# Low parts of streamed weight chunks: accumulating load onto the negated high part, in place of a subtraction

## The reference

```python
x = layer_norm(ALPHA * x + 0.5 * swiglu(x, ffn1_w_up, ffn1_w_down), ln1_g, ln1_b)
h, new_buf, S_new = mixer(x, ...)     # x @ w_in -> gates, short convolution, 4 retention heads,
                                      # y_conv = z @ w_conv_br, y_ret = o @ w_ret_br, m @ w_out
x = layer_norm(ALPHA * x + h, ln2_g, ln2_b)
x = layer_norm(ALPHA * x + 0.5 * swiglu(x, ffn2_w_up, ffn2_w_down), ln3_g, ln3_b)
```

## Time and profile before

| | us |
|---|---|
| median of 3 runs | 1780.68 (1778.77 to 1781.95) |
| span of the profiled execution | 1778.3 |
| stage: opening and first down product | 0 to 44.5 |
| rest of FFN 1 and its layer norm | 44.5 to 445 |
| quads of the input projection | 445 to 842 |
| last gates and convolution branch (chunks 32 to 42) | 842 to 932 |
| four heads (9 chunks each) | 932 to 1310 |
| output product, layer norm, first units of FFN 2 | 1310 to 1390 |
| rest of FFN 2, last layer norm | 1390 to 1778 |

### The profile page before, as it was taken

How to read it: one execution, slowest core, us unless ns; L and a number is a source line. 1 busy time by engine, 2 the same in 40 slices (tenths; PEclk the granted TensorE clock), 3 DMA queues, 4 the chain that set the end, 5 groups by cost and what they waited for, 6 DMA issues and landing times.

```text
span 1778.3 us, 26857 instructions
## 1 busy us (share of the span) xinstructions
PE 1766.5 (99%) x10776; PEld 1653.0 (93%) x10776; DVE 1286.1 (72%) x1708; ACT 653.3 (37%) x1120; POOL 551.6 (31%) x355
## 2 busy tenths in 40 slices
PE   9999999999999999999999999999999999999998
PEld 9989999898999999999998989898989989899997
DVE  7958485678788787777266777767867968485676
ACT  5425233243545454444105050514224325242343
POOL 3424242242232222221242323332343324233331
PEclk9999999999999999999999999999999999999999
DMA  7442423334443333433674858676963442324223
GB/s 275 136 137 72 143 78 130 126 94 178 148 148 127 115 128 99 139 98 95 243 247 159 313 198 296 214 265 222 351 264 118 129 154 86 131 79 135 90 89 107
DMA packets 87259, 282.61 MB, mean 159 GB/s; under 512 B 8672, under 2 KB 9056, under 8 KB 86880
## 3 DMA queue, kind: packets, MB, share of 16 engines
q1 hardware_dynamic: 48096, 172.77, 29.4%
q10 hardware_dynamic: 24784, 56.21, 8.7%
q0 software_dynamic: 14256, 51.91, 8.6%
HBM read 239.63 MB, written 42.28 MB: 159 GB/s over the span
## 4 chain that ended last, share of the span: by engine, by line
PE 94%; DVE 3%; DMA 1%; ACT 1%; issue 1%; DVEq 0%; ACTq 0%
PE ps L872 93%; PE ps L1348 1%; DMA out_ret_sample<-state 1%; DMA state<-in_state_ret 0%; DVE xl L1961 0%; DVE z L2277 0%; DMA opening<-in_opening 0%; DVE z L2380 0%; PE ps L1257 0%; DVE wql L1961 0%; ACT xh L1510 0%; ACT t L1900 0%; DVE t L2010 0%; DVE y L2415 0%; DVE tl L1961 0%
## 5 line engine op out<-in xcount | busy, mean ns | idle before, releaser
L872 PE MATMUL ps<-th,wql 128*128 128x320 f32 x1136 | 351.0, 309 | 0.0
L872 PE MATMUL ps<-th,wqh 128*128 128x320 f32 x1136 | 350.7, 309 | 0.0
L872 PE MATMUL ps<-tl,wqh 128*128 128x320 f32 x1136 | 350.0, 308 | 0.0
L773 POOL TENSOR_TENSOR wl<-raw,wh 128x1024 fp32r<-128x1024 f32 x100 | 262.8, 2628 | 133.9 <-DMA wh<-in_weights 81.8
L1510 ACT ACTIVATE pu<-ps 128x320 f32<-128x320 f32 x213 | 93.2, 438 | 515.8 <-PE ps L872 515.8
L1961 DVE TENSOR_TENSOR wql<-qraw,wqh 128x512 fp32r<-128x512 f32 x213 | 260.0, 1221 | 17.2 <-ACT wqh L1510 17.0
L872 PE MATMUL ps<-xh,wql 128*128 128x320 f32 x852 | 262.7, 308 | 0.2 <-DVE wql L1961 0.2
L872 PE MATMUL ps<-xl,wqh 128*128 128x320 f32 x852 | 262.7, 308 | 0.0
L872 PE MATMUL ps<-xh,wqh 128*128 128x320 f32 x852 | 262.6, 308 | 0.0
L786 POOL TENSOR_TENSOR quad_s<-qraw 128x512 f32<-128x512 f32 x71 | 96.7, 1362 | 478.8 <-DVE wql L1961 412.9
L1961 DVE TENSOR_TENSOR wql<-quad_s,wqh 128x512 fp32r<-128x512 f32 (+1 forms) x213 | 197.5, 927 | 44.2 <-ACT wqh L1510 43.4
(11 more groups left out here) (246 smaller groups left out, 3446.2 us busy)
## 6 DMA issues: line engine op xcount, KB each, us to landing
qraw<-in_quads SPq DMA_DIRECT2D x142, 512.0 KB, 3.6
raw<-in_weights SPq DMA_DIRECT2D x100, 512.0 KB, 3.9
wh<-in_weights POOLq DMA_DIRECT2D x92, 512.0 KB, 5.3
state<-in_state_ret ACTq DMA_DIRECT2D x32, 512.0 KB, 7.5
out_ret_sample<-state ACTq DMA_DIRECT2D x32, 512.0 KB, 6.4
state<-in_state_ret SPq DMA_DIRECT2D x16, 512.0 KB, 5.7
qk_scratch<-ctp SPq DMA_DIRECT2D x8, 640.0 KB, 5.6
swish_scratch<-ctp SPq DMA_DIRECT2D x6, 640.0 KB, 2.9
```

The costliest lines, as they stand in the source:

```text
L773: pool.tensor_tensor(w_lo(r), w_raw(r), w_hi(r).bitcast(f32), ALU.subtract).then_inc(chunk_split, 1)
L872: ins = nc.tensor.matmul(out, lhs, rhs, start=start, stop=stop, skip_group_check=adds)
```

## The change

For the 97 chunks that are not made by ScalarE, the plain load by SyncE is gone. GpSimd instead writes minus the high part into the low tile (a multiplication by -1), waits for that instruction's own semaphore, and issues a second load of the chunk with `accum_op=ALU.add` into the same tile: `-wh + w`. TensorE waits for the landing of that load (`low_loaded`, one semaphore per slot). `max_dma_last_dim=4 * D` lets one descriptor carry a row of 4 KB. SyncE no longer waits for the fourth chunk's plain load ahead of `z_scratch`, and ScalarE waits for the landing of chunk 25's low part ahead of the load of the norm's gains.

```diff
 def loads_of_slot(c):
-    return sum(SLOTS[e] == SLOTS[c] for e in range(FIRST_HI, c + 1))
+    return sum(SLOTS[e] == SLOTS[c] and e in BY_ACT for e in range(FIRST_HI, c + 1))
...
                 for _ in range(n):
                     c = ck.at
                     r = slot_of(c)
-                    slot_free(sync, c)
-                    sync.dma_start(w_raw(r), a["weights"][c]).then_inc(raw_loaded[r], 16)
+                    if c in BY_ACT:
+                        slot_free(sync, c)
+                        sync.dma_start(w_raw(r), a["weights"][c]).then_inc(raw_loaded[r], 16)
                     ck.add()
...
                 fourth = SECOND + FIRST_UNITS - 1
-                sync.wait_ge(raw_loaded[slot_of(fourth)], 16 * loads_of_slot(fourth))
...
                 c = ck.at
                 high(c + 1)
                 r = slot_of(c)
-                pool.wait_ge(raw_loaded[r], 16 * loads_of_slot(c))
                 if c in BY_ACT:
+                    pool.wait_ge(raw_loaded[r], 16 * loads_of_slot(c))
                     pool.wait_ge(hi_made, BY_ACT.index(c) + 1)
+                    pool.tensor_tensor(w_lo(r), w_raw(r), w_hi(r).bitcast(f32), ALU.subtract).then_inc(chunk_split, 1)
                 else:
                     pool.wait_ge(hi_loaded[r], 16 * high_loads_of_slot(c))
-                pool.tensor_tensor(w_lo(r), w_raw(r), w_hi(r).bitcast(f32), ALU.subtract).then_inc(chunk_split, 1)
+                    pool.tensor_scalar(w_lo(r), w_hi(r).bitcast(f32), -1.0, None, ALU.mult).then_inc(high_negated, 1)
+                    nk.add()
+                    pool.wait_ge(high_negated, nk())
+                    pool.dma_start(w_lo(r), a["weights"][c], accum_op=ALU.add,
+                                   max_dma_last_dim=4 * D).then_inc(low_loaded[r], 16)
                 ck.add()
...
             def chunk():
-                s = slot_of(ck.at)
+                c, s = ck.at, slot_of(ck.at)
                 ck.add()
-                if ck() > FIRST_HI:
-                    pe.wait_ge(chunk_split, ck(-FIRST_HI))
+                if c in BY_ACT:
+                    pe.wait_ge(chunk_split, BY_ACT.index(c) + 1)
+                elif c >= FIRST_HI:
+                    pe.wait_ge(low_loaded[s], 16 * high_loads_of_slot(c))
                 return s
...
-            act.wait_ge(chunk_split, FFN_CHUNKS - FIRST_HI)
+            act.wait_ge(low_loaded[slot_of(SECOND - 1)], 16 * high_loads_of_slot(SECOND - 1))
```

More of the change, by code:

```diff
@@ L485, in build_layer @@
         hi_loaded = [sem(f"hi_loaded{i}") for i in range(NSPL + 2)]
-        chunk_split = sem("chunk_split")
+        chunk_split, high_negated = sem("chunk_split"), sem("high_negated")
+        low_loaded = [sem(f"low_loaded{i}") for i in range(NSPL + 2)]
         first_loaded = [sem(f"first_loaded{n}") for n in range(len(FIRST_LOADS))]
@@ L751, in _ @@
         def _(pool):
-            ck, hk, qk = Count(FIRST_HI), Count(FIRST_HI), Count()
+            ck, hk, qk, nk = Count(FIRST_HI), Count(FIRST_HI), Count(), Count()
             def high(n):
```

## The result

The changed kernel takes **1933.41 us** (median, 1930.3 to 1934.81) against 1780.07 us: ratio **1.0858, interval 1.0843 to 1.0874**. The profiled execution has a span of 1930.9 us against 1778.3, so 152.6 us more. The forecast was 1865 us, range 1825 to 1940: the direction and the range held, the sum of 84 us was little more than half of what came.

The account below looks back on a forecast made before the run. TensorE, busy 99%, bounds the kernel, so new waits add to the span. Stage terms 2 + 1 + 8 + 24 + 44 + 5 = 84 us on 1778.3, plus 2.4 for the runs' median, gave 1865 us, range 1825 to 1940.

Parts of the forecast that it names:

- The bound and the room: TensorE busy 99%; in steady stretches 6.4 us from the next chunk's high-load issue to the low part's first use.
- The path, 7.4 us: Quiet DMA: issue 0.57, negation 1.3, semaphore 0.1, accumulating load 5.4 against 6.4 us of room, +1.0 us a chunk.
- The second limit: Accumulating load queued behind the next chunk's high load: 2.7 us after that lands, ready at 7.3 to 7.6 us.
- the queue costs more: Rival: accumulating load lands after 6.5 to 8 us alone, 3.5 to 4 behind another; 1906 to 1941, chance 0.27.
- Contention passes: Rival: only the quiet price holds, as slower TensorE spreads other transfers; +43 to 47, 1822 to 1828, chance 0.12.
- Busy DMA in the convolution branch: Full DMA engines from 868 to 905: 8.1 + 2.7 = 10.8 us against 6.4, +4.4 us a chunk; stage 24 us.
- The easing: Gates and convolution: slower chunks let other transfers finish in three chunks, not five; 20 instead of 26 us, 24 taken.
- the quiet price: Loss per chunk where DMA is not full: +1.0 us, taken as 1.1.
- Heads: Four heads: first chunk +5.9, second +3.8, then quiet ones of 1.1; 50 us, eased by a quarter 38, 44 taken.
- First layer norm: Chunk 26 +2.5, chunk 27 about +1, chunk 29 +4.4 us; sum +8, called the surest stage.
- FFN 2 and the opening: Opening +2 us at chunks 4 and 5; both FFNs +1 in all, tightest place covered by 1.1 us.
- The clock: Rival: waits of 4 to 6 us some fifteen times make the clock fall; +45, 1910 us, chance 0.06.

Follow-up runs that it names:

- e4: Kernel before, all its loads kept, GpSimd subtracting three times in a row for the 43 chunks of 33 to 79 not ScalarE's: 1879.61 us, ratio 1.0552.
- e2: Changed kernel with the second load of a chunk plain instead of accumulating, negation and its wait kept: 1878.07 us, ratio 1.0541.
- e9: Changed kernel with the negation covering 256 of 1024 columns in the three main slots, accumulating load whole: 1884.4 us, ratio 1.0583.
- e10: Changed kernel with a negation of 256 of 1024 columns in the main slots and a plain second load: 1834.17 us, ratio 1.0297.
- e8: Changed kernel with the accumulating load only for 33 chunks split well ahead of use, all others as before: 1780.34 us, ratio 0.9995.
- e11: Changed kernel with a negation of 16 of 1024 columns in the main slots, accumulating load whole: 1875.89 us, ratio 1.0525.
- e6: Changed kernel with 20 idle matmuls ahead of TensorE's wait for 26 chunks (projection's last units, convolution branch, heads): 1949.75 us, ratio 1.0942.

## Why the prediction was right in its direction and short in its sum

**The bound and the room: right.** TensorE at 99% could only lose. The room of 6.4 us is the right yardstick: a path of 7.9 us gives waits at every chunk in e4, where no transfer was touched, a shorter path gives time back in e2, e9 and e10, and e8, with accumulating loads where the room is wide, loses nothing.

**The path, 7.4 us: it was 9.5 us.** Term by term:
- Negation: taken 1.3 us, measured **2.80 us**. This is the term that was furthest off, and even my upper end of 2.4 us was too low. I had taken the subtraction as a bound from above, because it reads twice as much; nothing in the trace said that GpSimd's time goes by operands read. e9 prices it: 1.92 us less of it gives 49 us. Down to the 1.3 us that I took this would be, in proportion, some 38 us, over half of the 69 us that the sum lacked (an estimate from these two runs).
- Own semaphore: taken 0.1, measured 0.30 us, in every chunk.
- Accumulating load alone: taken 5.4, measured 6.0 (5.8 in the convolution branch). Nearly right; the store at the kernel's end was a fair stand-in, though it writes the other way.

**The second limit, one load behind another: the rule right, the price wrong.** I took 2.7 us behind the high load from the GB/s of the earlier trace rows, ready 7.3 to 7.6 us after the high load's issue. e11 measures 8.5 us, 4.1 behind. The engines alone were busy with one for 3.3 us; a mean rate over a window at the kernel's end did not show that. The rival "the queue costs more" had 3.5 to 4 us for this and a total of 1906 to 1941, in which the result lies (its stages add up to +122 to +153, so 1903 to 1934 would have been the right sum; those of "Contention passes" add up to 41 to 45, not 43 to 47); its other condition, a landing of 6.5 to 8 us alone, did not hold (6.0).

**Busy DMA in the convolution branch: about right for a few chunks.** I expected landings of 8 to 11 us and 4.4 us a chunk. Two landings took 9.5 and 9.1 us, with waits of 6.7 and 6.3 us and the DMA engines full in part of them (share 1.01 in 904:910 above); the chunk between them had its load after 5.3 us and did not wait. The high loads of this stretch, from 879.17 to 927.29, are 12.0 us apart in the mean, 5.0 more than before. Over the whole branch the landing was 5.8 us in the median, and plain high loads fell from 5.9 us before to 4.0. The easing that I wrote down, a slower TensorE spreads the other transfers, is real. The stage still lost 36 instead of 24 us, because the quiet price was 3.2 us a chunk and not 1.1: nine chunks at 3.2 make 29, and the two with the late landings some 7 more.

**Heads: 44 forecast, 83 measured**, the largest miss in microseconds, for the same reason. GpSimd's high loads give it chunk by chunk. In the first head, that of the earlier trace rows, they were 7.9, 7.0 and 7.1 us apart before and are 14.3, 12.9 and 8.4 apart now, and the step behind them grew by 4.3: 6.4 + 5.9 + 1.3 + 4.3 = 18. The next two lost 20 and 18; the last, up to the output product, 27. The first agrees with the 5.9 us forecast (the accumulating load lands after 9.7 us there), the second was forecast at 3.8, the rest at 2 to 3 in all; and the easing by a quarter that I took off did not come.

**First layer norm: 8 forecast, 10.4 measured, but at another chunk.** I had added three waits (chunks 26, 27, 29). There was one of size (and 0.4 us at 454.62):

```profile
451.71 1.70 PE L878 MATMUL ps<-xh,wl_x 128*128 128x320 f32 x5 [6.09 <-DMA wl_x<-in_weights]
```

It is for chunk 26, 2.5 us forecast. A wait at one chunk gives the next ones its own length as room, which is how I explain that waits at chunks split together did not add; no run tests it. Chunk 29 had enough. The size was about right because two errors met: one wait of the longest kind and 3.5 us of slow matmuls behind it.

**FFN 2 and the opening: 1 and 2 forecast (1 for both FFNs), 8.3 and 7.2 measured.** The place of the earlier trace rows itself did not stall, nor any other of FFN 1: a high load of 4.0 us, 2.8, 0.3 and 5.5 just fitted. Of the same places in FFN 2 one waited, 2.3 us at 1603.83, where the high load took 6.7 us to land. The other wait, 2.0 us at 1904.62, is at a place that the sum did not have: the last chunk, whose negation GpSimd starts only at 1895.58, behind VectorE's `ct`. In the opening chunk 4 waited 3.2 us and chunk 5 2.0. I had written that stalls in the FFNs would mean a landing over 6.5 us; they came with landings of 5.5 and 5.9, since the path's other parts were longer. With the negation at a quarter (e9) the two stages lose only 2.4 and 0.9 us.

**The clock.** It was a rival with a chance of 0.06 and nothing in the sum. The clock did fall behind such waits, 53 us of longer matmuls in all. That it is mostly hidden by the next wait was right for the loops (e6). It is not hidden at the last wait of a series: the four stages with single waits (opening, norms, FFN 2) carry 2.0 + 3.5 + 2.6 + 4.0 = 12 us of it, their difference less their waits of over 0.3 us. How much of the 13.5 and 26.7 us in convolution and heads is a loss of its own the runs do not separate.

## What to carry to other kernels

Before a short step is replaced by a chain (compute, semaphore, transfer), add up the chain from the event that starts it and compare it with the room between that event and the first use, chunk by chunk; where the chain is longer, and its start is released by the consumer, the excess returns with every chunk and the consumer runs at the chain's pitch. Price an operation that has no row by nothing that presumes what its time depends on: "reads less" bounded the negation from the wrong side. In this loop neither the emptier queue of SyncE, nor fillers for the clock, nor the one other order that was tried helped; only a shorter path, an earlier start, or using the new way where the room is wide did, and there it must still have something to give.

## What the runs showed of the hardware

- On GpSimd a multiplication by a constant, one operand, 128x1024 float32, took 2.80 us; the subtraction of two such operands takes 2.41 us. 256 columns took 0.88 us, 16 columns 0.28 us. The Trainium skill, "GPSIMD Engine Reference", section "4.1 Engine selection", calls an operation of one input roughly line-rate and one of two inputs about half as fast as VectorE's; by these rows the one-input operation is the slower one.
- From the end of a GpSimd instruction to the issue of a DMA behind a wait for its semaphore: 0.30 us, in 91 cases 27.5 us.
- An accumulating load of 512 KB of GpSimd's queue landed after 6.0 us (median of 92), its issue took 0.92 us; the plain one landed after 4.7 us in e2, with an issue of 0.58 us. Right behind another load the accumulating one took 7.4 us (e11, convolution branch). It kept all 16 DMA engines for 3.3 us, a plain one for 1.7 us (one load of each).
- Behind a wait of 6.25 us the granted clock was 0.50 and then 0.99 again; with a wait of 1.4 us at every chunk it stayed at 1.00 (e4, 865 to 912 us); in the kernel before it was 9 tenths or more in all 40 slices.
